# Twenty-four wide products between the small products of a delta rule's triangular levels

## The chip, the cores and the metric

The kernel runs on one core of a Trainium2 chip. The metric is the device time of one execution in microseconds. Before the change the median of three runs is 1872.4 us (1870.74 to 1874.98). Engine names are those of the profile: PE multiplies matrices, PEld is its weight load, DVE works elementwise, ACT applies functions and copies, POOL is the general engine, SP issues transfers.

## The reference, cut to what matters

The program is a two-part network over 256 tokens: an attention and expert block, then a block with a gated delta rule, a feed-forward layer, dilated attention and a second feed-forward layer. The change lies in the delta rule (eight heads, two directions). Its core, cut:

```python
a = jnp.where(strict, jnp.einsum('bhnid,bhnjd->bhnij', kb, k) * decay, 0.0)
rhs = jnp.concatenate([v * beta[..., None], kb * jnp.exp(G)[..., None]], axis=-1)
sol = lax.linalg.triangular_solve(a, rhs, left_side=True, lower=True, unit_diagonal=True)
...
v_new = u_c - jnp.einsum('bhck,bhkv->bhcv', w_c, state)
o_c = (jnp.einsum('bhck,bhkv->bhcv', qd_c, state) + jnp.einsum('bhij,bhjv->bhiv', intra_c, v_new))
state = (state * jnp.exp(gl_c)[..., None, None] + jnp.einsum('bhck,bhcv->bhkv', kd_c, v_new))
```

## The kernel before, in words

The kernel works with 32 triangular systems of 128 rows (8 heads, 2 directions, 2 blocks of tokens). It inverts each unit-triangular matrix from small blocks up. DVE solves all diagonal blocks of 32 rows at once (lines 2934 to 2943), then transposes the result twice (lines 2944 and 2945, each signals `leaf_side`). After that PE joins blocks in two levels:

- Level 5 joins 32-row blocks into 64-row blocks. `level5_e` (line 2607) multiplies 32x32 blocks into a bank, ACT copies the bank with a minus sign (`e_copy`, line 2831), `level5_d` (line 2616) multiplies again, and DVE puts the result into `VT` and `V` (`update`, lines 2957 to 2961, signals `half_done`). Two batches of 16 systems.
- Level 6 joins 64-row blocks into 128 rows: `level6_e` (line 2634), `wide_copy` on ACT (line 2839), `level6_d` (line 2642), and DVE's copies at lines 2972 and 2973 (`level_done`). Four batches of 8 systems, and on PE the order is e0, e1, d0, e2, d1, e3, d2, d3.

A product of 32-bit data is recorded as two matmul instructions, so one call of `level5_e` leaves 64 records, one of `level5_d` 96, and one of `level6_e` or `level6_d` 16. Both levels use all eight PSUM banks `ps[0]` to `ps[7]`: 0 and 1 for level 5's first products, 4 to 7 for its second, then `ps[batch]` and `ps[4 + batch]` in level 6. Behind the levels come products of 128x128 matrices with 128 columns (`products`, line 2677): three rounds of four groups (`v1`, `state`, `ks`), then line 2699 and a fourth round, then the read-out and the output projection (line 2739), then the feed-forward layer.

Each engine runs its own list in the order written, and they meet only at the semaphores. In front of the levels PE has the last half of a projection (`z_half(3, 1)`, line 2550) and then waits for `leaf_side`. ACT places blocks (`place`, line 2826) between its copies and has a conversion of weights (line 304) behind its last `wide_copy`. SP's weight transfers wait for `unit_done`, which PE signals at the end of each weight unit. `k.hT_hi`, rounded activations of the layer before, lies in memory and is read by nobody after POOL's sum at line 2522, until the next layer writes it.

Of the kernel before, what the change touches and what calls it, by code (L numbers as in the profile page):

```python
# [23 lines left out]
P = 128  # L24
# [1358 lines left out]
def flat(ap):  # L1383
    return ap.rearrange("p h s -> p (h s)")
# [1084 lines left out]
def gdn_solve(k, seam):  # L2469


    g, ps, U, H = k.gdn, k.ps, FIRST, GDN_H
# [38 lines left out]
    def rows(b, n=1):  # L2511
        return slice(b * B, (b + n) * B)
# [19 lines left out]
    def tensor(pe):  # L2532
# [74 lines left out]
        def level5_e(batch, bank):  # L2607

            for c in range(16):
                sys = 16 * batch + c  # L2610
                for to, of in blocks:
                    last = pe.matmul(bank[rows(to), c * B:(c + 1) * B], A[rows(of), sys, rows(to)],
                                     sideVT[rows(of), sys, :], start=True, stop=True)
            last.then_inc(e_mm, 1)

        def level5_d(batch, bank_t, bank):


            pe.wait_ge(e_out, batch + 1)
            for c in range(16):  # L2620
                sys = 16 * batch + c
                for to, of in blocks:
                    if to == 2 or c % 4 < 2:
                        pe.matmul(bank_t[rows(to), c * B:(c + 1) * B], sideV[rows(to), sys, :],
                                  side_E[batch][rows(to), c, :], start=True, stop=True)
            for c in range(16):
                sys = 16 * batch + c
                for to, of in blocks:
                    if to == 0 or c % 4 >= 2:
                        last = pe.matmul(bank[rows(of), c * B:(c + 1) * B], side_E[batch][rows(to), c, :],  # L2630
                                         sideV[rows(to), sys, :], start=True, stop=True)
            last.then_inc(d_mm, 1)

        def level6_e(batch, bank):

            for c in range(8):
                sys, to = 8 * batch + c, slice(c % 2 * Q, c % 2 * Q + Q)
                last = pe.matmul(bank[to, c // 2 * Q:(c // 2 + 1) * Q], A[Q:P, sys, 0:Q], VT[Q:P, sys, Q:P],
                                 start=True, stop=True)
            last.then_inc(wide_mm, 1)  # L2640

        def level6_d(batch, bank):

            pe.wait_ge(wide_out, batch + 1)
            for c in (0, 2, 1, 3, 4, 6, 5, 7):
                sys = 8 * batch + c
                at = slice(c * Q, (c + 1) * Q)
                if c % 4 < 2:
                    last = pe.matmul(bank[0:Q, at], V[0:Q, sys, 0:Q], wide_E[batch % 2][0:Q, c, :],
                                     start=True, stop=True)  # L2650
                else:
                    last = pe.matmul(bank[Q:P, at], wide_E[batch % 2][0:Q, c, :], V[0:Q, sys, 0:Q],
                                     start=True, stop=True)
            last.then_inc(last_mm, 1)

        pe.wait_ge(kq_out, 4)
        pe.wait_ge(leaf_side, 1)
        level5_e(0, ps[0])
        level5_e(1, ps[1])
        pe.wait_ge(z_out, 3)  # L2660
        pe.wait_ge(natural_out, H)
        pe.wait_ge(leaf_side, 2)
        level5_d(0, ps[4], ps[5])
        level5_d(1, ps[6], ps[7])
        pe.wait_ge(placed_VT, 1)
        pe.wait_ge(half_done, 1)
        for batch in range(4):
            if batch == 2:
                pe.wait_ge(half_done, 2)
            level6_e(batch, ps[batch])  # L2670
            if batch >= 1:
                level6_d(batch - 1, ps[4 + batch - 1])
        level6_d(3, ps[7])
# [238 lines left out]
    def vector(dve):  # L2912
# [113 lines left out]
        for n in range(4):  # L3026
# [9 lines left out]
            if n == 2:  # L3036
                split_lo(k, dve, U["mlp1_0"])
                seam.round_lo(dve, 1)
                seam.round_lo(dve, 2)

    return Stage(gpsimd=gpsimd, tensor=tensor, scalar=scalar, vector=vector)


# [848 lines left out]
```

## Time and profile before

| what | us |
|---|---|
| median of three runs | 1872.4 |
| the profiled execution's own time | 1869.39 |
| its span, first to last instruction | 1867.6 |
| PE busy | 1820.0 |
| DVE busy | 1263.9 |
| ACT busy | 950.8 |
| POOL busy | 318.8 |

The profiled execution lies 3.0 us under the median. Between its span and its own time lie 1.8 us. The granted clock is TensorE's: 1.00 is 2.4 GHz and 0.50 is 1.2 GHz, and its mean over the span is 0.994. A busy PE is not a PE at its peak, since matmuls are pipelined and their recorded spans overlap: the rate of a run of matmuls is read from the time between its first starts and its count, not from the mean length of one.

### The profile page before, as it was taken

Reading aid. Unit: us, or ns where it says so; the run is one execution under the profiler, and the core shown is the slowest. Engines: PE = TensorE matmul, PEld = TensorE weight load, DVE = VectorE, ACT = ScalarE, POOL = GpSimd, SP = SyncE. Lnnn points to the kernel's source line nnn. Section 1 sums busy time; section 2 is a strip of 40 time slices with the busy share of each in tenths; the row PEclk is TensorE's granted clock in tenths of the full one; section 3 lists DMA queues with packets and bytes.
Section 4 is the critical chain, followed back from the end, with each engine's and each line's share of the span. In section 5 each row is a group of like instructions: output and inputs, shape, how many; then the busy total and the mean of one; then the engine's idle time right before and its main releaser. Section 6 shows DMA issues by size and latency. Waiting matters only on the chain.

```text
span 1867.6 us, 29628 instructions
## 1 busy us (share of the span) xinstructions
PE 1820.0 (97%) x11949; PEld 1635.7 (88%) x11949; DVE 1263.9 (68%) x2143; ACT 950.8 (51%) x1326; POOL 318.8 (17%) x119
## 2 busy tenths in 40 slices
PE   7999999999999999999999999999999999989998
PEld 7999899999888888888888888888888889878887
DVE  5567875999677767655555557887577545757744
ACT  6457735544545544544444446676555333546533
POOL 0000002680566666500000000030000000100000
PEclk9999999999999999999999999998999999999999
DMA  6444345454443434465555554321145457635543
GB/s 237 160 162 159 135 181 203 159 184 178 158 158 136 158 140 154 147 225 197 186 201 184 198 194 150 136 91 69 48 181 196 163 194 226 179 115 209 184 169 147
DMA packets 44756, 310.60 MB, mean 166 GB/s; under 512 B 5183, under 2 KB 5695, under 8 KB 8161
## 3 DMA queue, kind: packets, MB, share of 16 engines
q1 hardware_dynamic: 42592, 303.58, 44.9%
q0 software_dynamic: 1472, 4.86, 1.4%
q8 instruction: 81, 1.33, 0.3%
q10 hardware_dynamic: 576, 0.55, 0.1%
q14 instruction: 35, 0.28, 0.0%
HBM read 306.84 MB, written 2.13 MB: 165 GB/s over the span
## 4 chain that ended last, share of the span: by engine, by line
PE 60%; DVE 14%; POOL 5%; ACT 4%; issue 1%; ACTq 0%; DVEq 0%
PE bank L1738 18%; PE bank L3114 9%; PE bank L347 7%; PE bank L377 6%; POOL s_ring_lo L1895 5%; PE bank L381 3%; PE bank L360 3%; PE bank L364 3%; ACT s_w_hi L304 3%; DVE s_arena L1907 1%; PE bank L3373 1%; DVE s_ring_lo L310 1%; PE bank L465 1%; PE bank L2739 1%; PE bank L1709 1%
## 5 line engine op out<-in xcount | busy, mean ns | idle before, releaser
L304 ACT ACTIVATE s_w_hi<-s_ring 128x2048 fp32r<-128x2048 f32 x244 | 465.9, 1909 | 132.2 <-PE bank L347 42.0
L310 DVE TENSOR_TENSOR s_ring_lo<-s_ring,s_w_hi 128x2048 fp32r<-128x2048 f32 x183 | 418.7, 2289 | 140.5 <-ACT s_w_hi L304 135.9
L1895 POOL TENSOR_TENSOR s_ring_lo<-s_ring,s_w_hi 128x2048 fp32r<-128x2048 f32 x62 | 286.0, 4613 | 497.9 <-ACT s_w_hi L304 494.9
L1738 PE MATMUL bank<-s_w_hi,s_h_r 128*128 128x512 f32 x1008 | 239.0, 389 | 1.4 <-issue 1.3
L1738 PEld LDWEIGHTS bank<-s_w_hi,s_h_r 128*128 128x128 f32 x1008 | 189.0, 188 | 41.2 <-issue 1.9
L347 PE MATMUL bank<-s_h_r,s_w_hi 128*128 128x256 f32 x1664 | 218.7, 284 | 0.3 <-DVE s_arena L3602 0.3
L347 PEld LDWEIGHTS bank<-s_h_r,s_w_hi 128*128 128x128 f32 x1664 | 207.0, 192 | 4.8 <-issue 3.6
L360 PE MATMUL bank<-s_h_r,s_w_hi 128*128 128x512 f32 x704 | 180.2, 398 | 0.0
L360 PEld LDWEIGHTS bank<-s_h_r,s_w_hi 128*128 128x128 f32 x704 | 126.2, 189 | 22.6
L1852 ACT ACTIVATE s_h_r<-s_arena 128x512 fp32r (+1 forms) x64 | 40.4, 632 | 183.5 <-PE bank L1738 183.4
L3086 DVE TENSOR_TENSOR s_ring_lo<-s_ring,s_spare_r 128x2048 fp32r<-128x2048 f32 x32 | 73.1, 2291 | 77.3 <-ACT s_spare_r L3072 77.1
L1738 PE MATMUL bank<-s_ring_lo,s_h_r 128*128 128x512 f32 x504 | 124.5, 389 | 0.0
L377 PE MATMUL bank<-s_h_r,s_w_hi 128*128 128x512 f32 x480 | 120.4, 393 | 0.0
L3114 PE MATMUL bank<-s_spare_r,s_mid_r 128*128 128x512 f32 x512 | 119.7, 390 | 0.0
L347 PE MATMUL bank<-s_h_r,s_ring_lo 128*128 128x256 f32 x832 | 116.9, 283 | 1.4 <-DVE s_ring_lo L310 1.4
L3114 PEld LDWEIGHTS bank<-s_spare_r,s_mid_r 128*128 128x128 f32 x512 | 95.8, 188 | 20.3 <-issue 0.3
L1738 PEld LDWEIGHTS bank<-s_ring_lo,s_h_r 128*128 128x128 f32 x504 | 94.6, 188 | 19.7
L347 PEld LDWEIGHTS bank<-s_h_r,s_ring_lo 128*128 128x128 f32 x832 | 107.3, 192 | 1.8 <-DVE s_ring_lo L310 1.8
L364 PEld LDWEIGHTS bank<-s_h_r,s_ring_lo 128*128 128x128 f32 x704 | 94.3, 190 | 16.3 <-POOL s_ring_lo L1895 10.9
L2051 DVE TENSOR_TENSOR s_h_r<-s_arena,s_h_r 128x512 fp32r<-128x512 f32 x64 | 46.1, 720 | 90.9 <-ACT s_h_r L1852 90.9
L3072 ACT ACTIVATE s_spare_r<-s_ring 128x2048 fp32r<-128x2048 f32 x32 | 61.1, 1916 | 87.4 <-DMA s_ring<-weights 87.4
L364 PE MATMUL bank<-s_h_r,s_ring_lo 128*128 128x256 f32 x704 | 100.3, 285 | 1.8
(473 smaller groups left out, 2825.0 us busy)
## 6 DMA issues: line engine op xcount, KB each, us to landing
s_ring<-weights SPq DMA_DIRECT2D x282, 1024.0 KB, 4.8
s_arena<-bias_by_distance POOLq DMA_DIRECT2D x12, 384.0 KB, 8.1
s_arena<-mem SPq DMA_DIRECT2D x1, 1024.0 KB, 5.9
s_x<-x SPq DMA_DIRECT2D x1, 1024.0 KB, 13.4
x_away<-s_x SPq DMA_DIRECT2D x1, 1024.0 KB, 8.1
s_arena<-sub_keys SPq DMA_DIRECT2D x1, 1024.0 KB, 11.5
s_arena<-x_away SPq DMA_DIRECT2D x1, 1024.0 KB, 7.0
out<-s_x SPq DMA_DIRECT2D x2, 512.0 KB, 2.6
```

Of the source, the lines that this page charges most:

```text
L304: act.activation(k.w_hi[:, u % 2, :], k.ring[:, u % RING, :], ACT.Copy).then_inc(k.hi_ready, 1)
L310: dve.tensor_tensor(k.ring_lo[:, u % RING, :], k.ring[:, u % RING, :], plain(k.w_hi[:, u % 2, :]), ALU.subtract).then_inc(k.lo_ready, 1)
L347: last = pe.matmul(out[:, nb * S:(nb + 1) * S], w[:, c, nb * P:(nb + 1) * P], h[:, c, :], start=(n == 0 and c == 0), stop=(n == 2 and c == 7))
L360: pe.matmul(banks[nb][:, :], hi[:, c, nb * P:(nb + 1) * P], h_swapped[:, :, c, :], start=(c == 0), stop=False)
L364: last = pe.matmul(banks[nb][:, S:2 * S], lo[:, c, nb * P:(nb + 1) * P], h_hi[:, c, :], start=False, stop=(c == 7))
L377: pe.matmul(banks[nb][:, :], hi[:, c, nb * P:(nb + 1) * P], h_both[:, :, c, :], start=(c == 0), stop=False)
L381: last = pe.matmul(banks[nb][:, 0:S], lo[:, c, nb * P:(nb + 1) * P], h_hi[:, c, :], start=False, stop=(c == 7))
L1738: last = pe.matmul(ps[4 + 2 * tt + dh][:, :], g[:, b, tt * P:(tt + 1) * P], w[:, b, dh * 512:(dh + 1) * 512], start=(d == 0 and n == 0 and ...
L1895: pool.tensor_tensor(k.ring_lo[:, u % RING, :], k.ring[:, u % RING, :], plain(k.w_hi[:, u % 2, :]), ALU.subtract).then_inc(k.lo_ready, 1)
L3072: act.activation(wide_hi[:, u % RING], slot(k, u), ACT.Copy).then_inc(k.hi_ready, 1)
L3086: dve.tensor_tensor(lo, w, plain(wide_hi[:, u % RING]), ALU.subtract).then_inc(k.lo_ready, 1)
L3114: last = pe.matmul(ps[4 + 2 * pair + tt][:, :], m[:, 8 * q + c, tt * P:(tt + 1) * P], w[:, c, at, :], start=(q == 0 and n == 0 and c == 0) ...
```

## The change

A helper `wide_products(bank, count)` issues `count` products of one stationary 128x128 block of `k.hT_hi` with 512 columns of `k.hT_hi`, into one bank. Nobody reads the results, and nothing is signalled. Nine go to `ps[2]` ahead of the wait for `leaf_side`. Fifteen stand between the small products: one after `level5_e(0)`, two after `level5_e(1)`, three after each `level5_d`, all to `ps[2]`, and two after each of `level6_e(0)`, `(1)` and `(2)`, to `ps[3]`. Both banks are overwritten later by level 6 (`ps[2]` by `level6_e(2)`, `ps[3]` by `level6_e(3)`). No wait is added or taken away.

```diff
--- before.py
+++ after.py
@@ -2653,21 +2653,35 @@
                                      start=True, stop=True)
             last.then_inc(last_mm, 1)
 
+        def wide_products(bank, count):
+
+
+            rounded = flat(k.hT_hi[:, 0:4, :])
+            for n in range(count):
+                pe.matmul(bank[:, :], rounded[:, 0:P], rounded[:, 512:1024], start=True, stop=True)
+
         pe.wait_ge(kq_out, 4)
+        wide_products(ps[2], 9)
         pe.wait_ge(leaf_side, 1)
         level5_e(0, ps[0])
+        wide_products(ps[2], 1)
         level5_e(1, ps[1])
+        wide_products(ps[2], 2)
         pe.wait_ge(z_out, 3)
         pe.wait_ge(natural_out, H)
         pe.wait_ge(leaf_side, 2)
         level5_d(0, ps[4], ps[5])
+        wide_products(ps[2], 3)
         level5_d(1, ps[6], ps[7])
+        wide_products(ps[2], 3)
         pe.wait_ge(placed_VT, 1)
         pe.wait_ge(half_done, 1)
         for batch in range(4):
             if batch == 2:
                 pe.wait_ge(half_done, 2)
             level6_e(batch, ps[batch])
+            if batch < 3:
+                wide_products(ps[3], 2)
             if batch >= 1:
                 level6_d(batch - 1, ps[4 + batch - 1])
         level6_d(3, ps[7])
```

## Rows read from the trace of the kernel before

**Rows 1.** the page: busy share of the span, and the chain that ended last, by engine

```profile
PE 1820.0 (97%) x11949; PEld 1635.7 (88%) x11949; DVE 1263.9 (68%) x2143; ACT 950.8 (51%) x1326; POOL 318.8 (17%) x119
...
PE 60%; DVE 14%; POOL 5%; ACT 4%; issue 1%; ACTq 0%; DVEq 0%
```

**Rows 2.** busy time, with granted clock (PEclk), in stretches of the rule and after it

```profile
core 0: us, PE busy (x) PEld busy (x) DVE busy (x) ACT busy (x) POOL busy (x), PEclk, DMA share, GB/s
1280.00:1282.25 2.25, 0.17 (x1) 0.00 (x0) 2.18 (x3) 1.32 (x2) 0.00 (x0) 1.00 0.34 58
1282.25:1284.00 1.75, 1.67 (x105) 1.70 (x107) 1.72 (x2) 0.35 (x1) 0.00 (x0) 1.00 0.98 412
1284.25:1291.50 7.25, 6.89 (x210) 6.65 (x203) 2.63 (x5) 4.07 (x6) 0.00 (x0) 0.50 0.05 19
1291.50:1298.50 7.00, 6.98 (x137) 6.60 (x132) 4.69 (x10) 5.23 (x11) 0.00 (x0) 0.50 0.02 5
1298.50:1301.25 2.75, 2.75 (x16) 2.63 (x14) 2.52 (x6) 1.47 (x3) 0.00 (x0) 0.50 0.00 0
1301.50:1304.50 3.00, 3.00 (x29) 3.00 (x29) 3.00 (x6) 2.65 (x10) 0.00 (x0) 1.00 0.00 0
```

**Rows 3.** PE in order of time: start, us, engine, line, operation, count, [idle before <-releaser]

```profile
1276.55 3.62 PE L2550 MATMUL bank<-s_hT,s_ring 128*128 128x256 f32 x16
1282.33 2.33 PE L2612 MATMUL bank<-s_arena 32*32 32x32 f32 x128 [2.16 <-DVE s_arena L2944]
1284.98 1.76 PE L2624 MATMUL bank<-s_arena 32*32 32x32 f32 x45 [0.32 <-ACT s_arena L2831]
...
1291.67 1.97 PE L2638 MATMUL bank<-s_arena 64*64 64x64 f32 x32
```

**Rows 4.** PE in order of time behind the levels: the products of line 2677 and next

```profile
1298.38 0.31 PE L2652 MATMUL bank<-s_arena 64*64 64x64 f32 x1
1298.62 12.26 PE L2677 MATMUL bank<-s_arena 128*128 128x128 f32 x96
1310.71 3.74 PE L2699 MATMUL bank<-s_arena 128*128 128x128 f32 x32
```

**Rows 5.** ACT in order of time in the levels

```profile
1283.65 1.19 ACT L2831 ACTIVATE s_arena<-bank 32x512 f32<-32x512 f32 x2 [2.33 <-PE bank L2612]
...
1285.93 1.19 ACT L2831 ACTIVATE s_arena<-bank 32x512 f32<-32x512 f32 x2
...
1292.84 0.77 ACT L2839 ACTIVATE s_arena<-bank 64x256 f32<-64x256 f32 x2 [4.43 <-PE bank L2638]
1293.63 0.62 ACT L2826 ACTIVATE s_arena<-s_arena 32x512 f32<-32x512 f32 x1
```

**Rows 6.** DVE in order of time in the levels

```profile
1288.84 0.69 DVE L2957 COPY s_arena<-bank 32x512 f32<-32x512 f32 x1 [4.18 <-PE bank L2630]
...
1290.67 0.43 DVE L2961 COPY s_arena<-bank 32x256 f32<-32x256 f32 x1
1291.80 0.69 DVE L2957 COPY s_arena<-bank 32x512 f32<-32x512 f32 x1 [0.70 <-PE bank L2630]
...
1295.78 0.42 DVE L2972 COPY s_arena<-bank 64x256 f32<-64x256 f32 x1 [1.72 <-ACT s_arena L2826]
```

**Rows 7.** busy time and granted clock in four other stretches, columns as in group 2

```profile
1480.00:1510.00 30.00, 30.00 (x134) 24.86 (x133) 13.06 (x8) 9.26 (x6) 0.00 (x0) 1.00 0.53 203
225.00:228.00 3.00, 0.12 (x2) 0.00 (x0) 2.71 (x2) 0.84 (x2) 0.00 (x0) 1.00 0.55 169
...
229.50:232.75 3.25, 3.25 (x18) 3.25 (x17) 3.25 (x4) 2.75 (x2) 0.00 (x0) 0.51 0.00 0
1647.80:1651.00 3.20, 0.00 (x0) 0.00 (x0) 3.13 (x5) 0.77 (x1) 0.00 (x0) 1.00 0.00 0
```

**Rows 8.** PE's waits from 1300 us to the end, longest first: total, times, longest

```profile
PE bank L3373 <- DVE s_mid_r L3586: 5.2, 2, 3.4
PE bank L2728 <- DVE s_arena L3014: 2.1, 3, 1.5
```

## The prediction, made before the changed kernel was run

> **What bounds the kernel now.** I read the page first. PE is busy 97% of the span and holds 60% of the chain that ended last [rows 1], so as a rule a microsecond taken from PE's list is a microsecond of the kernel. Then I read the granted clock along the span. It has one long dip, and the change lies in it. PE idles from 1280.2 us to 1282.33, with 0.17 us busy in 2.25 us, still at 1.00; the first small products still run at 1.00; from 1284.25 on the clock is 0.50, and it stays there through both triangular levels although PE is busy 6.89 of 7.25 and 6.98 of 7.00 us [rows 2]. It comes back only after 2.75 us of products with the full 128x128 array, and is 1.00 again from 1301.5 [rows 2]. The reader is to see two things: busy time alone does not bring the clock back, and PE is the engine that is slow there. Last I read the order of time on PE, ACT and DVE, to see what waits for what.
>
> **What the small products cost at either clock.** `level5_e` leaves 128 records between 1282.33 and about 1284.5, nearly all at full clock [rows 3], which is 17 ns for each record. `level5_d` leaves 192 records between 1284.98 and 1291.67 at half clock [rows 3], 35 ns for each. Level 6 is 128 records in 7.0 us, 54 ns [rows 2, 3], so I take 27 ns at full clock. The 128x128 products run at 16 records in 2.75 us at half clock [rows 2], with a few missing, and at full clock at about 112 ns each (32 records of line 2699 in 3.74 us, of which some 0.17 is the drain of the last) [rows 4]. So halving the clock doubles all four.
>
> **What a wide product costs.** In the feed-forward layer 134 products of 512 columns fill 30 us at 1.00 [rows 7], 0.22 us each. At half clock that is 0.44 us.
>
> **The nine ahead.** The last product of line 2550 is issued by about 1280.0 (16 records over 3.5 us from 1276.55) [rows 3]. Nine wide products are 9 x 0.22 = 1.98 us, up to 1282.0. PE's next work starts at 1282.33, released by DVE's transpose [rows 3]. They cost nothing: the wait for `leaf_side` hides them, with 0.3 us to spare. At half clock they would take 4.0 us and be 1.7 us late, but the clock there is 1.00 [rows 2]. No wait is added anywhere, and SP and POOL are moved past nothing.
>
> **The fifteen between**, if the clock stays at 1.00. I follow the chain:
> - `level5_e(0)` 64 x 0.017 = 1.09 us, one wide 0.22, `level5_e(1)` 1.09, two wide 0.44: PE is free at 1285.2. ACT's first copy does not move (1283.65 to 1284.84), so `level5_d(0)` starts at 1285.2 instead of 1284.98: 0.2 us lost.
> - `level5_d(0)` 96 x 0.017 = 1.63 us, to 1286.8; three wide, to 1287.5. ACT's second copy ends at 1287.12 [rows 5], as before, so `level5_d(1)` runs to 1289.1 and three wide to 1289.8.
> - DVE's update is 2.26 us (1288.84 to 1291.10) [rows 6]. Both follow each other: 1287.0 to 1289.3 to 1291.55. Before, the second ended near 1294.06 (1291.80 + 2.26).
> - Level 6: `level6_e` 16 x 0.027 = 0.43 us, so e0, two wide, e1, two wide run from 1289.8 to 1291.5. ACT's copy of 0.77 us [rows 5] and its placing of 0.62 us [rows 5] alternate, 1.4 us for each batch, and these now set the pace: copies end at 1291.2, 1292.6, 1294.0 and 1294.8. So most of the six wide products here fall into waits of PE. `level6_d(3)` ends at 1295.3.
> - The first product of line 2677 starts at 1295.3 instead of 1298.62 [rows 4]; DVE's `level_done` (0.42 and 0.43 us per group [rows 6]) comes from 1294.0 on and is not late.
> This is 3.3 us. The second term: 96 records of line 2677 take 1298.62 to 1310.71, 12.1 us [rows 4], of which 2.6 us ran at half clock [rows 2]; at full clock they take 10.8 us, 1.3 us less. Together 4.6 us.
>
> **What I can't read.** No row shows a full-array product between small ones at full clock. The nearest row is the change from the last 64x64 product to the first 128x128: starts at 1298.38 and 1298.62 at half clock [rows 4], 0.24 us against 0.11 us for a normal pair, so up to 0.07 us more at full clock, twice for each of six insertions: 0 to 0.8 us. A gain is excluded, since nothing is taken out. I take 0.2 us, because half of the insertions end in a wait. The sum is 4.6 - 0.2 = 4.4 us.
>
> The Trainium skill, "TensorE: Matmul & The Clock Gate", section "The mechanism", says that a weight load overlaps running matmuls only when their row groups differ. A wide product uses all row groups, so by this rule each insertion drains the array, and the sum would be 3.8 us, with the upper bound of the switch.
>
> **Whether it goes through to the end.** Behind line 2677 PE waits little: the largest waits after 1300 us are 5.2 and 2.1 us in total [rows 8], both for results of a chain that moves along with PE. The weights' transfers are started by units that PE finishes, and nothing on PE waits for a transfer there. So I pass the 4.4 us on in full: 1869.39 - 4.4 = 1865.0 for an execution like the profiled one. The median of the runs is 3.0 us above that execution, and I forecast the median: 1872.4 - 4.4 = 1868.0 us.
>
> **The rivals.**
> 1. *The clock stays up* (the sum): 1868.0. For it: between 1282.0 and 1289.8, where there were only small products, now six wide ones stand (1.3 us of full-array work), and in level 6 six more; the clock also stayed at 1.00 through an idle stretch of 3.2 us (1647.8 to 1651.0) and fell after a 3.0 us one (225 to 228) only later, at 229.5 [rows 7], so a stretch that looks too empty is not always punished. Chance 0.5.
> 2. *It falls later, or falls in some executions and not in others.* The trace has idle stretches of the same length with and without a fall [rows 7], so where the fall comes depends on more than the work. If it falls near 1290 and returns soon behind 1298, level 5 is fast, the last six wide products take 0.44 us, and I get a first product of line 2677 near 1298 to 1299 and an end of its 96 records at 1310.3: -0.4 us. A mixture of both has a median 1 to 3 us faster: about 1871. Against it: the density of full work rises in level 6. Chance 0.3.
> 3. *It falls as before and the wide products are paid at half clock.* The small ones then weigh as little as they did, and the added ones are too few. The place is PE's list from 1284.25 to 1298.5, where PE has no idle time to hide them (6.98 of 7.00 us busy [rows 2]). One stands before the fall; 14 x 0.44 = 6.2 us. Slower by 6 us: 1878; with the fall at 1287.5 it is +2.7 us: 1875. The point from which it decides is a fall before about 1290: there the six or more products left cost as much as the time won. Chance 0.2.
>
> A fourth, that the levels are bound by ACT and DVE anyway, so that a fast PE brings less, is in the sum: without wide products at full clock the chain would start line 2677 at 1294.7, only 0.6 us earlier than with them.
>
> The Trainium skill, "TensorE: Matmul & The Clock Gate", section "What's actually happening", says that the clock follows how busy PE has been recently. The row of 1284.25 to 1298.5, busy and at 0.50, does not agree with that read as busy time; by that rule the nine products alone would do all the work and the fifteen only cost, and the sum would be the same or better by their 0.6 us.
>
> **How the numbers follow.** The likeliest case gives 1868.0. Its own range is 1865 to 1870, from the switch cost (0 to 0.8 us) and the spread of the runs shown. The range goes over to case 2 and to the milder part of case 3: 1864.5 to 1875.5, which leaves out the full price of case 3. What a measurement of this kernel can tell from no change is about 0.2%, 3.7 us. Case 1 passes this bound with 0.85, case 2 with 0.15: 0.47 faster. Case 3 passes it on the other side with 0.75: 0.15 slower. The rest is 0.38.
>
> **What would show it.** Right: a granted clock of 1.00 from 1282 to 1302, `level5_d`'s 192 records in some 4 us with the six wide ones among them, the first 128x128 product at 1295.3 to 1296, and 96 of them in 10.8 us. PE's wait for `leaf_side` is down to 0.2 to 0.4 us. Wrong: a stretch at 0.50 with wide products of 0.44 us in it; or a clock of 1.00 and the first product of line 2677 later than 1297, which would be the switch cost; or an earlier start whose gain is lost again before line 2739.

## The result, and the profile after

The changed kernel takes 1879.96 us (median of 13 runs, 1873.96 to 1883.65) against 1872.99 us before (13 runs, 1869.33 to 1876.89). The ratio is 1.0035 with a 95% interval of 1.0027 to 1.0043: 6.6 us slower by the ratio, 7.0 us by the medians. The forecast was 4.4 us faster, and the measured time lies outside its range.

The changed kernel's profiled execution took 1877.12 us, 7.7 us more than that of before. First, its busy time in stretches, with granted clock (columns: stretch and its length, busy time with count of PE, PEld, DVE, ACT and POOL, granted clock, DMA share, GB/s):

```profile
1280.75:1283.25 2.50, 2.42 (x11) 1.65 (x9) 2.42 (x4) 1.48 (x2) 0.00 (x0) 1.00 0.29 69
1283.25:1288.50 5.25, 5.04 (x205) 4.24 (x206) 2.44 (x2) 3.77 (x6) 0.00 (x0) 1.00 0.41 170
1288.75:1295.75 7.00, 7.00 (x123) 5.51 (x118) 3.52 (x6) 0.63 (x2) 0.00 (x0) 0.50 0.02 5
1295.75:1306.50 10.75, 10.38 (x135) 7.65 (x134) 3.43 (x9) 5.35 (x11) 0.00 (x0) 0.50 0.01 2
1306.50:1308.75 2.25, 2.25 (x12) 2.25 (x11) 2.09 (x5) 0.97 (x2) 0.00 (x0) 0.50 0.00 0
1309.25:1318.50 9.25, 9.25 (x85) 9.25 (x84) 7.93 (x17) 6.82 (x17) 0.00 (x0) 1.00 0.01 2
```

Set beside [rows 2], the idle stretch in front of the levels is filled: PE is busy 2.42 of 2.50 us with the nine products. The clock, which was 0.50 from 1284.25 on, is now 1.00 to 1288.5. Then it falls all the same, in the middle of level 5, and is 0.50 through the rest of both levels and 2.25 us of the 128x128 products. The half-clock time did not get shorter: it is some 20 us (1288.5 to 1309) against 17 before (1284.25 to 1301.25 [rows 2]). It moved back, and wide products now stand in it.

The chain of work through the levels tells what each piece cost (start, duration, engine and line; 2612 is `level5_e`, 2624 and 2630 `level5_d`, 2638 `level6_e`, 2661 the wide products):

```profile
1283.30 1.20 PE bank L2612 x64
1284.50 0.43 PE bank L2661
1284.94 1.13 PE bank L2612 x64
1286.07 0.66 PE bank L2661 x2
1286.73 0.91 PE bank L2624 x39
...
1289.42 1.58 PE bank L2661 x3
1291.00 1.69 PE bank L2624 x45
...
1294.37 1.58 PE bank L2661 x3
1295.95 1.05 PE bank L2638 x16
1297.00 1.15 PE bank L2661 x2
```

One wide product took 0.43 us and two 0.66 us at full clock; three took 1.58 us at half clock, twice, and two took 1.15 us at half clock, the first of three such groups. The fifteen cost 0.43 + 0.66 + 2 x 1.58 + 3 x 1.15 = 7.7 us of the chain. The weight load of the small product behind a group starts only as the last wide product ends:

```profile
1290.93 1.68 PEld L2624 LDWEIGHTS bank<-s_arena 32*32 32x32 f32 x46 [0.65 <-issue]
```

Behind the levels PE's list is what it was:

```profile
1306.50 12.17 PE L2691 MATMUL bank<-s_arena 128*128 128x128 f32 x96
1318.51 3.74 PE L2713 MATMUL bank<-s_arena 128*128 128x128 f32 x32
```

96 records from 1306.50 to 1318.51 are 12.0 us, against 12.1 before [rows 4]. From the first small product to the first 128x128 product it is 23.2 us (1283.30 to 1306.50) against 16.3 us (1282.33 to 1298.62 [rows 3, 4]). That is 6.9 us of the 7.7 us that lie between the two executions. The rest was there before the levels began, at 1283.30 instead of 1282.33: near 230 us this execution was at half clock for 6.8 us, where the profile of before has 3.4 us [rows 7], and already the projection in front of the nine (line 2550) starts at 1277.46 instead of 1276.55 [rows 3].

```profile
227.25:233.75 6.50, 5.78 (x27) 5.81 (x28) 6.18 (x5) 4.24 (x3) 0.00 (x0) 0.50 0.32 134
```

### The profile page after: what moved, and what is told of

Same layout as the page of the kernel before. It is cut to its first block, busy times and chain, and to the rows that moved or that the text cites. A ratio compares the mean times of both kernels' runs of the same rounds, so it can differ in the third digit from the quotient of the medians.

```text
span 1875.3 us, 29675 instructions
## 1 busy us (share of the span) xinstructions
PE 1829.1 (98%) x11973; PEld 1640.4 (87%) x11973; DVE 1264.6 (67%) x2143; ACT 950.8 (51%) x1326; POOL 318.8 (17%) x119
## 4 chain that ended last, share of the span: by engine, by line
PE 60%; DVE 13%; POOL 5%; ACT 4%; issue 1%; ACTq 0%; DVEq 0%
PE bank L1738 18%; PE bank L3128 9%; PE bank L347 7%; PE bank L377 6%; POOL s_ring_lo L1895 5%; PE bank L381 3%; PE bank L360 3%; PE bank L364 3%; ACT s_w_hi L304 2%; DVE s_arena L1907 1%; PE bank L3387 1%; DVE s_ring_lo L310 1%; PE bank L1709 1%; PE bank L465 1%; PE bank L2753 1%
## 5 line engine op out<-in xcount | busy, mean ns | idle before, releaser
L1738 PEld LDWEIGHTS bank<-s_ring_lo,s_h_r 128*128 128x128 f32 x504 | 94.7, 188 | 19.6
L364 PEld LDWEIGHTS bank<-s_h_r,s_ring_lo 128*128 128x128 f32 x704 | 94.3, 190 | 16.3 <-POOL s_ring_lo L1895 10.9
## 6 DMA issues: line engine op xcount, KB each, us to landing
s_x<-x SPq DMA_DIRECT2D x1, 1024.0 KB, 13.6
```

Source lines behind the costliest of these rows:

```text
L364: last = pe.matmul(banks[nb][:, S:2 * S], lo[:, c, nb * P:(nb + 1) * P], h_hi[:, c, :], start=False, stop=(c == 7))
L1738: last = pe.matmul(ps[4 + 2 * tt + dh][:, :], g[:, b, tt * P:(tt + 1) * P], w[:, b, dh * 512:(dh + 1) * 512], start=(d == 0 and n == 0 and ...
```

## The experiments

For each run two lengths are read from its profile and used below. *Levels* is the time from the first record of `level5_e` to the first 128x128 product. *Behind* is from there to the first product of the read-out (line 2711 of the kernel before). In the two profiles above levels is 16.3 and 23.2 us and behind is 19.2 and 19.2 us.

| kernel | ahead, between | median us | ratio to before, 95% interval | levels | behind | clock in the levels |
|---|---|---|---|---|---|---|
| before | 0, 0 | 1873 | | 16.3 | 19.2 | falls |
| changed | 9, 15 | 1880.0 | 1.0035 (1.0027 to 1.0043) | 23.2 | 19.2 | falls |
| before, second profile | 0, 0 | 1875.8 (one) | | 16.25 | 20.7 | falls |
| changed, second profile | 9, 15 | 1873.1 (one) | | 16.35 | 18.0 | 1.00 |
| nine only | 9, 0 | 1873.5 | 1.0000 (0.9990 to 1.0011) | 15.9 | 19.6 | falls |
| fifteen only | 0, 15 | 1883.4 | 1.0059 (1.0044 to 1.0073) | 25.1 | 19.8 | falls |
| twenty-eight | 9, 28 | 1876.9 | 1.0022 (1.0013 to 1.0031) | 18.8 | 18.0 | 1.00 |
| 32x32 tiles | 9, 28 | 1886.3 | 1.0065 (1.0050 to 1.0081) | 29.2 | 19.5 | falls |
| 32 columns | 9, 28 | 1882.7 | 1.0052 (1.0037 to 1.0067) | 23.3 | 20.6 | falls |
| no nine | 0, 28 | 1882.4 | 1.0066 (1.0041 to 1.0090) | 25.9 | 18.0 | falls, comes back |
| three more | 9, 18 | 1873.4 | 1.0004 (0.9995 to 1.0013) | 16.5 | 18.0 | 1.00 |
| lean | 9, 14 | 1871.9 | 1.0000 (0.9986 to 1.0014) | 15.7 | 18.0 | 1.00 |
| lean b | 9, 14 | 1871.5 | 0.9994 (0.9985 to 1.0003) | 15.4 | 18.0 | 1.00 |
| lean c | 9, 12 | 1870.9 | 0.9995 (0.9984 to 1.0006) | 20.3 | 19.4 | falls |

The last three columns are those of one profiled execution each. For the other executions only the mean clock over the span is known. It is 0.994 to 0.997 in the five profiles whose clock holds in the levels and 0.987 to 0.994 in the nine whose clock falls there (0.994 in the first of before), so 0.995 or more speaks for a clock that held, 0.992 or less for one that fell, and 0.993 and 0.994 decide nothing.

**Nine only.** The fifteen between are taken out.

```diff
         wide_products(ps[2], 9)
         pe.wait_ge(leaf_side, 1)
         level5_e(0, ps[0])
-        wide_products(ps[2], 1)
         level5_e(1, ps[1])
-        wide_products(ps[2], 2)
...
-        wide_products(ps[2], 3)
...
-        wide_products(ps[2], 3)
...
-            if batch < 3:
-                wide_products(ps[3], 2)
```

> Only the nine wide products ahead of the wait stay; the fifteen between the small products are gone. Theory A (the clock needs work of the full array; the small products count for little, so nine products can only delay the fall): the clock falls within about 3.5 us of where it fell before, is at 0.50 for 17 to 20 us, and the time is that of before within 0.1%: 1872 to 1874 us. Theory B (the idle wait of 2.2 us in front of the levels is what makes the clock fall): no dip in the rule, 4 to 5 us faster than before: about 1868 us.

It takes the time of before, 1873.5 us. The stretches of its trace, columns as above:

```profile
1281.00:1283.50 2.50, 2.50 (x12) 1.79 (x10) 2.40 (x4) 1.66 (x2) 0.00 (x0) 1.00 0.23 46
1283.50:1289.25 5.75, 4.57 (x240) 4.30 (x241) 2.59 (x3) 4.11 (x7) 0.00 (x0) 1.00 0.41 168
1289.50:1299.50 10.00, 9.74 (x207) 9.15 (x205) 6.87 (x14) 5.61 (x12) 0.00 (x0) 0.50 0.01 3
```

PE has no idle stretch in front of the levels, and the clock falls at 1289.3, 5.6 us after the levels begin, instead of 1.9 us. So theory B falls, the wait is not what the clock needs to fall, and theory A holds in the main: the nine cost nothing, as predicted, and delay the fall without bringing time. In two details it misses: the fall comes 5 us later than before, not within 3.5, and the clock is back at 1302.9, after 13.6 us and not 17 to 20. And this is worth noticing: 4 us less at half clock in the levels made them only 0.4 us shorter (15.9 against 16.3). In the part that now runs at full clock PE waits 0.45 us for ACT's copy and is idle for another 0.60 us inside `level5_d(0)`.

**Fifteen only.** The nine ahead are taken out.

```diff
         pe.wait_ge(kq_out, 4)
-        wide_products(ps[2], 9)
         pe.wait_ge(leaf_side, 1)
```

> Only the fifteen wide products between the small ones stay; the nine ahead are gone, so PE idles again in front of the levels. Theory A: dip as before, and nearly all of the fifteen are paid at half clock with a price of 0.53 us each (3 in 1.58 us in the changed kernel): 7 to 8 us slower than before, 1880 to 1881 us, as slow as the changed kernel or 1 us slower. Theory C (it is the nine that cost, by delaying the release of the levels): the time of before, 1873 us.

```profile
1280.00:1282.25 2.25, 0.14 (x1) 0.00 (x0) 2.18 (x4) 1.29 (x2) 0.00 (x0) 1.00 0.38 66
1284.00:1307.00 23.00, 22.63 (x394) 17.80 (x396) 7.64 (x15) 9.26 (x18) 0.00 (x0) 0.50 0.04 13
1307.50:1311.00 3.50, 3.50 (x18) 3.50 (x17) 3.40 (x7) 1.67 (x4) 0.00 (x0) 0.50 0.00 0
```

It takes 1883.4 us, 2 to 3 us more than theory A expected and 3.4 us more than the changed kernel. PE idles again (0.14 of 2.25 us busy) and the clock is 0.50 for 27 us, from 1284 to 1311.2. All the loss of the change is in the fifteen, none in the nine, which win back some 3 us of it. Theory C falls.

**Twenty-eight between.**

```diff
         level5_e(0, ps[0])
-        wide_products(ps[2], 1)
+        wide_products(ps[2], 3)
         level5_e(1, ps[1])
-        wide_products(ps[2], 2)
+        wide_products(ps[2], 4)
...
-        wide_products(ps[2], 3)
+        wide_products(ps[2], 6)
...
-        wide_products(ps[2], 3)
+        wide_products(ps[2], 6)
...
-                wide_products(ps[3], 2)
+                wide_products(ps[3], 3)
```

> Nine ahead and 28 between instead of 15 (3, 4, 6, 6 in level 5 and 3, 3, 3 in level 6). Theory A: enough full-array work for the clock to stay at 1.00 from the wait to the 128x128 products; each wide product then costs 0.22 us and each group 0.26 us for the switch (1.57 us from level5_e(0) to level5_e(1) in the changed kernel, with 1.09 us of small products and one wide), so PE needs 12.3 us for small products and 28 wide ones at 0.22 us and 7 switches: the first 128x128 product comes 16 to 17 us after the release and the 96 take 10.8 us: 1 us faster to 1 us slower than before. Theory D (nothing put between small products holds the clock, because it is the presence of the small ones that lets it fall): half clock again and 28 at 0.53 us: 15 us slower, 1888 us.

```profile
1281.00:1302.25 21.25, 20.54 (x487) 16.06 (x485) 11.73 (x19) 11.00 (x20) 0.00 (x0) 1.00 0.15 52
```

The clock is 1.00 from before the levels to their end, and the twelve executions have a mean clock over their spans of 0.993 to 0.997, where the 29 of before measured beside them have 0.988 to 0.994. Theory D falls: enough full-array work does hold the clock in the levels. This run also gives the prices at full clock that the trace of before could not, in PE's order of time:

```profile
1287.73 1.10 PE L2624 MATMUL bank<-s_arena 32*32 32x32 f32 x45
...
1289.77 1.66 PE L2661 MATMUL bank<-s_h_r 128*128 128x512 f32 x6
1291.36 1.10 PE L2624 MATMUL bank<-s_arena 32*32 32x32 f32 x45
...
1294.98 0.68 PE L2638 MATMUL bank<-s_arena 64*64 64x64 f32 x16
1295.60 0.97 PE L2661 MATMUL bank<-s_h_r 128*128 128x512 f32 x3
1296.49 0.68 PE L2638 MATMUL bank<-s_arena 64*64 64x64 f32 x16
...
1302.25 0.94 PE L2691 MATMUL bank<-s_arena 128*128 128x128 f32 x6
```

The 96 records of `level5_d` take 2.04 us (1287.73 to 1289.77); at half clock they take 3.37 us (1291.00 to 1294.37 in the chain of the changed kernel). `level6_e` takes 0.62 us (1294.98 to 1295.60) against 1.05 us. Six wide products take 1.59 us (1289.77 to 1291.36) and three take 0.89 us (1295.60 to 1296.49), so one is 0.23 us and a group costs 0.2 us more for the change between small and full tiles. Levels is 18.8 us, above the 16 to 17 us expected, and 28 are too many: the kernel is slower than before by 0.22%. Of that, levels and behind explain only 1.2 us (36.8 against 35.5 us); the rest of some 3 us must lie outside them, see below.

**Lean.** Fourteen between, in fewer groups.

```diff
         level5_e(0, ps[0])
-        wide_products(ps[2], 1)
         level5_e(1, ps[1])
-        wide_products(ps[2], 2)
+        wide_products(ps[2], 4)
...
             if batch < 3:
-                wide_products(ps[3], 2)
+                wide_products(ps[3], (0, 2, 2)[batch])
```

> Nine ahead and 14 between, placed where PE would wait or where they form fewer groups: none after level5_e(0), 4 after level5_e(1), 3 after each level5_d, 0, 2 and 2 in level 6. [...] Theory D: 7 us slower.

With one product less than the changed kernel it is 8 us faster, at 1871.9 us, the time of before within the interval. It has fewer wide products in all and in level 6, and one more in front of `level5_d(0)`. The clock stays at 1.00 in the profiled execution, and ten of twelve executions have a mean clock of 0.995 to 0.997; the other two have 0.992 and 0.989 and take 1877.4 and 1883.1 us. PE in order of time:

```profile
1286.59 0.95 PE L2624 MATMUL bank<-s_arena 32*32 32x32 f32 x38
1288.09 0.34 PE L2624 MATMUL bank<-s_arena 32*32 32x32 f32 x7 [0.55 <-issue]
...
1299.03 2.16 PE L2690 MATMUL bank<-s_arena 128*128 128x128 f32 x17
```

Levels is 15.7 us (1283.31 to 1299.03), where 13.5 to 14.5 us were expected of a clock that holds. One part is plain here: an idle 0.55 us inside `level5_d(0)`, for which the profile shows no wait ("issue"). An idle of 0.14 to 0.6 us stands in every profile whose `level5_d(0)` starts at full clock within 3.6 us of the first small product, and in neither of the two that start it there at full clock 4 us or more after (*twenty-eight* and *three more*). Its cause was not looked for.

**32x32 tiles.** The kernel with twenty-eight, with the products on one 32x32 tile.

```diff
-                pe.matmul(bank[:, :], rounded[:, 0:P], rounded[:, 512:1024], start=True, stop=True)
+                pe.matmul(bank[0:32, :], rounded[0:32, 0:32], rounded[0:32, 512:1024], start=True, stop=True)
```

> The 28 + 9 products of the run with 28, in the same places and with the same 512 columns, but on one 32x32 tile of the array instead of the full 128x128 (stationary 32x32, 32 rows of output). Theory A1 (what counts for the clock is how much of the array works): the clock is 0.50 from within 3.5 us of the first small products on, each product costs 0.4 to 0.45 us, and the time is 10 to 14 us above before: 1883 to 1887 us. Theory A2 (what counts is that columns are streamed at all, or that PE has no gap): the clock stays at 1.00 as with the full array, 1875 to 1877 us.

```profile
1284.25:1300.00 15.75, 15.75 (x273) 10.57 (x272) 4.95 (x9) 4.10 (x7) 0.00 (x0) 0.50 0.03 9
```

PE is busy 15.75 of 15.75 us with the same number of columns streamed, and the clock is 0.50: it fell at 1284.2, where it fell before, and stays at 0.50 to 1314.9, 3.3 us into the 128x128 products. The time is 1886.3 us. Theory A2 falls. Neither a gapless PE nor streamed columns hold the clock in this kernel; work of the whole array does.

**32 columns.** The same places, full array, 32 columns.

```diff
-                pe.matmul(bank[:, :], rounded[:, 0:P], rounded[:, 512:1024], start=True, stop=True)
+                pe.matmul(bank[:, 0:32], rounded[:, 0:P], rounded[:, 512:544], start=True, stop=True)
```

> The 28 + 9 products in the same places on the full array, but with 32 columns instead of 512, so that little but the weight loads and the changes between small and full tiles is left. The clock falls as in the kernel before. Theory S (a change between tiles costs 0.2 to 0.3 us for a group at either clock): 7 groups cost 2 us and the 28 weight loads another 2 to 3 us at half clock: 3 to 5 us slower than before, about 1877 us. Theory N (changes are free, as the prediction nearly took them): at most 1 us slower, 1873 to 1874 us.

```profile
1284.34 0.51 PE L2661 MATMUL bank<-s_h_r 128*128 128x32 f32 x3
1284.78 1.92 PE L2612 MATMUL bank<-s_arena 32*32 32x32 f32 x64
...
1290.96 1.35 PEld L2661 LDWEIGHTS bank<-s_h_r 128*128 128x128 f32 x6
1290.96 1.46 PE L2661 MATMUL bank<-s_h_r 128*128 128x32 f32 x6
1292.35 1.76 PE L2624 MATMUL bank<-s_arena 32*32 32x32 f32 x45
...
1298.16 0.82 PE L2661 MATMUL bank<-s_h_r 128*128 128x32 f32 x3
1298.91 1.12 PE L2638 MATMUL bank<-s_arena 64*64 64x64 f32 x16
```

```profile
1284.75:1306.50 21.75, 21.37 (x410) 20.30 (x409) 7.81 (x16) 9.77 (x18) 0.00 (x0) 0.50 0.03 13
```

The clock falls at 1284.7, about as in the kernel before, so instructions on the full array with few columns do not hold it either. Three cost 0.44 us at full clock (1284.34 to 1284.78). At half clock six cost 1.39 us and three 0.75 us: 0.21 us for each and 0.1 us for the group. So products with 1/16 of the columns cost nearly half of the wide ones at half clock. PE's weight load is busy for 1.35 of the 1.39 us of the six, so it is the weight loads that are paid. The time is 1882.7 us, 9.5 us above before: more than theory S expected, and theory N, which the prediction nearly took, falls. The change of tiles alone is the smaller part, 0.1 us at half clock here. With 512 columns it is 0.2 us at full clock (the run with twenty-eight) and 0.3 us at half clock (1.58 us for three, 1.15 us for two in the changed kernel).

**No nine.** The kernel with twenty-eight, without the nine ahead (the edit is that of *fifteen only*).

> The 28 between stay, the nine ahead are gone, so that PE idles 2.2 us and then runs the 1.1 us of level5_e(0) before the first wide product. Theory A: this stretch of 3.3 us nearly without full-array work is as thin as the one that let the clock fall before, so it falls in a part or most of the executions, and comes back within the levels since the 28 are dense enough: 1 to 6 us above the run with all 37: 1878 to 1883 us. Rival: the nine do nothing, the same time as with them, 1877 us.

```profile
1283.00:1285.25 2.25, 0.18 (x1) 0.00 (x0) 2.18 (x4) 1.34 (x2) 0.00 (x0) 1.00 0.35 66
1285.25:1286.75 1.50, 1.36 (x65) 1.35 (x66) 1.50 (x1) 0.04 (x1) 0.00 (x0) 1.00 0.96 404
1287.25:1303.75 16.50, 16.50 (x274) 13.20 (x272) 4.91 (x9) 4.12 (x7) 0.00 (x0) 0.50 0.02 8
1304.25:1311.00 6.75, 6.17 (x131) 4.61 (x129) 2.21 (x6) 4.62 (x11) 0.00 (x0) 1.00 0.01 2
```

After 2.2 us of idle PE the first small product runs at full clock, and from 1287.0 the clock is 0.50 until 1304.0, where it comes back while level 6 runs, before any 128x128 product. So the wide products can also bring it back, but the 28 need some 17 us for it; with the same products on 32x32 tiles it did not come back ahead of the 128x128 ones. Two executions have a mean clock of 0.993, three 0.985 to 0.991, and the median is 5.4 us above that with the nine. Two of the five, at 1890.1 and 1892.1 us, lie above the range expected. The nine do their part, which *nine only* could not show.

**Three more.** One edit of the changed kernel: three products more in one place.

```diff
         level5_e(1, ps[1])
-        wide_products(ps[2], 2)
+        wide_products(ps[2], 5)
```

> The changed kernel with one edit: five wide products after level5_e(1) instead of two, 18 between in all. Theory A (the changed kernel is too thin in full-array work in one place, from the small products of level5_e to the end of level5_d(0), and the clock falls for that): the clock now stays at 1.00 in most executions, and the kernel with three more useless products is 4 to 7 us faster than the changed one: 1873 to 1876 us. Theory E (the changed kernel is too thin everywhere between, in level 6 as well): it falls all the same, perhaps a few us later: 1879 to 1882 us.

```profile
1283.71 1.20 PE L2612 MATMUL bank<-s_arena 32*32 32x32 f32 x64
...
1285.27 1.20 PE L2612 MATMUL bank<-s_arena 32*32 32x32 f32 x64
1286.40 1.42 PE L2661 MATMUL bank<-s_h_r 128*128 128x512 f32 x5
1287.75 1.10 PE L2624 MATMUL bank<-s_arena 32*32 32x32 f32 x45
...
1300.19 9.98 PE L2691 MATMUL bank<-s_arena 128*128 128x128 f32 x87
```

```profile
1283.25:1302.00 18.75, 18.04 (x484) 14.50 (x483) 11.46 (x21) 11.36 (x20) 0.00 (x0) 1.00 0.14 56
```

The kernel with eighteen takes 1873.4 us, 6.6 us less than the one with fifteen by the medians and 5.8 us less by the ratios to before. The three cost 0.7 us and the clock is 1.00 in the profile; nine of the eleven executions have a mean clock of 0.995 or 0.996 and two 0.994, against 0.989 to 0.992 in eleven of thirteen of the changed kernel. Theory A holds and theory E falls: the changed kernel is too thin in full-array work in one place, from the first small product to the end of `level5_d(0)`. By itself this run would also allow that three more anywhere do it, since no run adds three elsewhere. *Lean* above and *lean c* below speak against that: they have one and three fewer than the changed kernel in all, but four instead of three in front of `level5_d(0)`, in one group, and most of their executions hold.

**Lean b and lean c.** 0, 5, 3, 1 in level 5 and 0, 3, 2 in level 6; and 0, 4, 3, 0 and 0, 3, 2.

> Nine ahead, 14 between, as 0, 5, 3, 1 in level 5 and 0, 3, 2 in level 6. Compared with the version of 0, 4, 3, 3 and 0, 2, 2 two products move from behind level5_d(1), where they delay level6_e(0) and with it ACT's chain of copies, to places where PE waits. Theory A: if the clock holds, the first 128x128 product comes 14.7 to 15.2 us after the release instead of 15.7, and the median is 1870 to 1871 us, 2 to 3 us under before; the risk is a fall in more executions, since the stretch of level5_d(1) has less full-array work: then single executions of 1877 to 1883 us. Theory D': nothing below 1872 us, since what level 6 wins is lost behind it.

> Nine ahead, 12 between: 0, 4, 3, 0 in level 5 and 0, 3, 2 in level 6. Theory A: where the clock holds, the first 128x128 product comes 14.6 to 15 us after the release and the time is 1868 to 1870 us; without any wide product behind level5_d(1) the stretch from there to level 6 is thin, and the clock falls in a third or more of the executions, which then take 1875 to 1880 us. The median is 1870 to 1873 us, and the spread is larger than with 14.

Medians of 1871.5 and 1870.9 us, 1.6 and 2.1 us below before, with intervals that include no change. Levels of lean b is 15.4 us, not 14.7 to 15.2, and its slowest execution, of 1876.8 us, has a mean clock of 0.993. In lean c eight executions take 1869.1 to 1871.1 us with a mean clock of 0.996 or 0.997, and three take 1875.0 to 1880.5 us with 0.990 to 0.993; its profile is the slowest of them. No version was shown to beat the kernel before.

**Both kernels once more.** Neither is changed.

> The kernel before, unchanged, profiled once more. The other kernels show short stretches at half clock outside the levels (near 228, 1157, 1337, 1654 and 1670 us), the first profile of before only the one at 229.5. Theory P (these belong to the program and come and go from execution to execution): a second profile of before shows some of them too, with its dip in the levels of 14 to 17 us, starting 2 to 6 us after the release of the levels. Theory Q (they come only where the levels' dip is gone or moved): before shows the one near 229 and no other.

> The changed kernel, unchanged, profiled once more. The clock falls again in level 5, between 1.5 and 6 us after the release, and stays at half for 14 to 21 us; the stretch from the release to the first 128x128 product takes 20 to 23.5 us (23.2 in its first profile) against 16.3 before.

The second profile of before falls in the levels 1.5 us after they begin and for 20.5 us, both outside what was expected, and has short half-clock stretches of 3.4 us near 1158, 1168 and 1656 us as well as at 229; the first had only the last. Theory P holds in its main point: they come and go with the execution. Levels is 16.25 us, as before, and behind is 20.7 us, 1.4 us more than in the first profile. The second profile of the changed kernel is against what was expected: the clock did not fall in the levels at all. Its chain of work:

```profile
1288.08 0.89 PE bank L2661 x3
...
1292.15 0.61 PE bank L2638 x16
1292.76 0.66 PE bank L2661 x2
```

The same three wide products now take 0.89 us, two take 0.66 us and `level6_e` 0.61 us. Levels is 16.35 us (1282.30 to 1298.65) and behind 18.0 us. So the changed kernel is a mixture. Of its 13 timed executions, those of 1873.96 and 1875.75 us have a mean clock of 0.995 and 0.994, the other eleven 0.989 to 0.992. When the clock holds, 1873.1 us was measured: no slower than before, of which an execution beside it took 1873.3 us, and no faster either. Levels and behind are 1.2 us shorter than in the first profile of before, but the rest of the kernel is 5 us longer, with 10 us of half clock near 1650 and 1667 us, where that profile has none:

```profile
1649.50:1656.00 6.50, 5.66 (x26) 5.67 (x27) 5.65 (x10) 3.80 (x8) 0.00 (x0) 0.50 0.00 1
```

## Why the prediction was wrong

**The choice of the likeliest case.** Rival 1, the clock stays up, got 0.5, and rival 3, it falls and the wide products are paid at half clock, 0.2. What came is rival 3, with rival 2's mixture around it. Rival 3's mechanism was right as written: a stretch at 0.50 with the wide products in it. Its price was too small: 2.7 us with the fall at 1287.5, and measured are 6.9 us with a fall at 1288.5. At its own prices the fifteen would cost 12 x 0.44 + 3 x 0.22 = 5.9 us there, so it let the later fall win back some 3.2 us. Measured, they cost 7.7 us and 0.8 us came back; *nine only*, with a fall 3.7 us later in the levels, won 0.4 us. The step that failed is the argument for rival 1, "six wide ones stand between 1282.0 and 1289.8", which counted wide products over a stretch and did not ask how they lie in it. Only three stand ahead of `level5_d(0)`, beside 2.3 us of small products and in front of the 2 us of `level5_d(0)` itself, and the clock falls at its end. *Three more* shows what this place does: six instead of three there, and the clock holds; the two lean versions, with fewer in all, point at the same place. The other half of the argument, that an idle stretch is not always followed by a fall [rows 7], is true and fits an outcome that differs between executions; it was no evidence for one side.

**The nine ahead** were put at no cost, hidden by the wait. Right: *nine only* has the time of before.

**The price of a wide product.** Forecast 0.22 and 0.44 us, with 0 to 0.07 us for each change of tile. Measured for a group of n at full clock: 0.23 n + 0.2 us. At half clock three cost 1.58 and two 1.15 us, 0.43 each and 0.3 us for the group. The product was right. The change of tile was put at 0.2 us for all insertions together and is 0.2 us for each; even the upper bound, twice 0.07 us for each, was too low. The prediction also counts six insertions where the kernel has seven, so this term is 1.4 us at full clock and not 0.2. The Trainium skill, "TensorE: Matmul & The Clock Gate", section "The mechanism", says that weight loads overlap running matmuls only across different row groups; the trace agrees only at the end of a group, where the next weight load starts at 1290.93, as the last wide product ends at 1291.00. Within a group it does not: the weight load of the group's third product starts at 1289.95, as the second product starts on the same rows, and the third product follows 0.42 us later. The sum that the prediction drew from the rule, 3.8 us, was nearer but still far off.

**Halving the clock doubles the small products.** Wrong, and the rows did not show it: they have each kind of small product at one clock only. `level5_d` is 2.04 and 3.37 us, a factor of 1.65; `level6_e` 0.62 and 1.05 us, 1.7. At full clock the 17 ns read from `level5_e` was carried over to `level5_d`, which has 21 ns, and level 6 was halved from 54 to 27 ns, where `level6_e` by itself has 39 ns. What a full clock can win in the levels was therefore too large.

**The term behind the levels**, 1.3 us for the 128x128 products. Right (1.2 us): behind is 18.0 us in every profile whose clock is at 1.00 by then, and 19.2 us in the two profiles compared, where it is not (19.4 to 20.7 us in the other six).

**That the rest passes on in full.** Right for the two profiles compared, with luck: from the first product of the read-out to the end of the span it is 549.7 us in both (1317.9 to 1867.6 and 1325.6 to 1875.3). In the other twelve it is 551.0 to 555.0 us, and it grows with the half-clock time between 1330 and 1700 us: none in these two, 13.6 us in the one with 555.0. These 5 us are more than the whole win that was forecast.

**The sum of rival 1, had it come.** The prediction has levels at 13.0 us (1282.33 to 1295.3) and thus -3.3 us. The changed kernel with the clock held has 16.35 us, no less than the 16.3 of before. Level 6 began 9.85 us after the first small product and not 7.5: `level5_d(0)` came 0.5 us late, the two batches of `level5_d` took 2.4 and 2.3 us and not 1.63, idle moments included, and the two groups of three 0.5 us more together. Level 6 itself took 6.5 us and not 5.5, with a wait of 0.6 us for ACT near its end. So 4.4 us would have been 1.2 us even in the best case, which is less than a measurement of this kernel can tell from no change: a second error, hidden behind the first.

**A rule about busy time.** The Trainium skill, same page, section "What's actually happening", says that the clock follows how busy PE has been recently. Read as busy time it does not agree: PE was busy 15.75 of 15.75 us at 0.50 in the run with 32x32 tiles, and at 1.00 in the same places with full tiles.

**What stays open.** Why an execution falls or holds at the same work: the profiles show where, not why. And whether a kernel that keeps its clock in the levels is more often at half clock elsewhere: the run with twenty-eight is 4.0 us above before where its levels and behind account for 1.2 us of their two profiles, and *three more* is 0.4 us above where they account for 1.1 us less. Half-clock stretches stand behind the levels in both profiles (from about 1337, 1654 and 1671 us in the first, from 1651 and 1668 us in the second). But the five profiles that hold have 3.4 to 13.6 us of them between 1330 and 1700 us, the nine that fall 0 to 10.2 us: they overlap, and fourteen profiles do not decide it.

## What to carry to other kernels

Small-tile products leave the clock to fall however busy they keep PE; full-array products put between them can hold it, but they must be dense enough in the thinnest place, and a sprinkling below that is paid at half clock (15 products: 6.6 us slower, 18: no change). Price a remedy in both states before believing in one, with its tile changes, and take the gain at full clock from measured rows, not from half of the slow ones. Products put where PE waits anyway are free, and here they also brought nothing alone. Ask, too, what a faster engine will wait for: in this kernel 4 us less at half clock was worth 0.4 us.

## What the hardware showed that was not expected

- The same kernel on the same inputs held its clock in one execution and lost it in another: levels of 16.35 and 23.2 us, 1873.1 and 1877.1 us in all.
- 32-column products on the full array cost 0.21 us each at half clock, against 0.43 us for 512 columns.
- An idle 0.14 to 0.6 us inside a run of 32x32 products at full clock, with no wait in the profile, which ends 4.3 to 4.8 us after the first small product (six profiles; its cause is open).
